# Entry of a two-block transformer kernel: the input rows and the first weight block in other pieces, and another order of the first roundings

## The reference

```
def rms_norm(x, g):
    y = xf * lax.rsqrt(jnp.mean(xf * xf, axis=-1, keepdims=True) + EPS)
    return (y * g.astype(jnp.float32)).astype(x.dtype)

def swiglu(h, w_gate, w_up, w_down):
    return (jax.nn.silu(h @ w_gate) * (h @ w_up)) @ w_down

x = x + 0.5 * swiglu(rms_norm(x, ffn1_norm[l]), ffn1_w_gate[l], ffn1_w_up[l], ffn1_w_down[l])
```

## Time and profile before

| what | value |
|---|---|
| median of 3 runs | 2433.48 us |
| profiled execution: its time, its span | 2435.74 us, 2434.0 us |
| TensorE busy | 2372.3 us, 97% |
| GpSimd, ScalarE, VectorE busy | 47%, 35%, 34% |
| share of TensorE in the chain that ended last | 88% |

### The profile page before, as it was taken

The page is one execution under the profiler, slowest core; times in us unless marked ns, Lnnn a source line. Parts: engine busy times, 40 slices in busy tenths (PEclk is TensorE's granted clock), DMA queues, the critical chain, the costliest instruction groups (busy, mean ns, idle before and its releaser), DMA issues.

```text
span 2434.0 us, 27037 instructions
## 1 busy us (share of the span) xinstructions
PE 2372.3 (97%) x11178; PEld 1930.8 (79%) x11178; DVE 821.5 (34%) x1415; ACT 855.4 (35%) x1260; POOL 1148.8 (47%) x936
## 2 busy tenths in 40 slices
PE   8999999999999999999997899999999899999999
PEld 6888887888877888888884678888876678788887
DVE  3222205754222221201568542021048864410210
ACT  4222215414343322213446443133165353531330
POOL 6444446525655444444551364444456521644443
PEclk9999999999999999999999999999999899999999
DMA  4323223212332332233230032332222201322232
GB/s 146 102 89 104 88 103 107 89 48 87 121 104 75 98 99 92 87 105 103 71 103 19 18 104 87 104 92 96 95 78 70 69 1 49 91 92 98 87 104 86
DMA packets 147132, 210.65 MB, mean 87 GB/s; under 512 B 6201, under 2 KB 112962, under 8 KB 147010
## 3 DMA queue, kind: packets, MB, share of 16 engines
q1 hardware_dynamic: 147010, 208.93, 26.7%
HBM read 206.82 MB, written 2.10 MB: 86 GB/s over the span
## 4 chain that ended last, share of the span: by engine, by line
PE 88%; DVE 7%; ACT 2%; issue 2%; DMA 1%; POOL 0%; SPq 0%; DVEq 0%; ACTq 0%
PE ps L1400 27%; PE ps L1402 26%; PE ps L1401 26%; PE ps L2157 1%; DVE c_work L2856 1%; DVE c_best L2855 1%; PE ps L2133 1%; PE ps L2143 1%; DVE hl L2292 1%; PE ps L1719 1%; PE ps L1741 1%; PE ps L1651 1%; DVE small L2716 0%; PE ps L2079 0%; DVE c_w L2662 0%
## 5 line engine op out<-in xcount | busy, mean ns | idle before, releaser
L757 POOL TENSOR_TENSOR wlo<-raw,whi 128x512 fp32r<-128x512 f32 x776 | 1010.2, 1335 | 1123.8 <-ACT whi L895 1007.5
L895 ACT ACTIVATE whi<-raw 128x2048 fp32r<-128x2048 f32 x189 | 360.1, 1905 | 699.6 <-DMA raw<-in_mlp_w 319.6
L1400 PE MATMUL ps<-hh,whi 128*128 128x512 f32 x1448 | 573.3, 396 | 6.9 <-DVE hl L2292 4.9
L1401 PE MATMUL ps<-hl,whi 128*128 128x512 f32 x1448 | 566.8, 391 | 0.0
L1402 PE MATMUL ps<-hh,wlo 128*128 128x512 f32 x1448 | 566.6, 391 | 0.0
L1400 PEld LDWEIGHTS ps<-hh,whi 128*128 128x128 f32 x1448 | 273.7, 189 | 75.5 <-DVE hl L2292 9.0
L1402 PEld LDWEIGHTS ps<-hh,wlo 128*128 128x128 f32 x1448 | 273.7, 189 | 57.8
L1401 PEld LDWEIGHTS ps<-hl,whi 128*128 128x128 f32 x1448 | 273.8, 189 | 56.9 <-issue 1.2
L1400 PE MATMUL ps<-gh,whi 128*128 128x512 f32 x736 | 286.3, 389 | 0.0
L1401 PE MATMUL ps<-gl,whi 128*128 128x512 f32 x736 | 286.3, 389 | 0.0
L1402 PE MATMUL ps<-gh,wlo 128*128 128x512 f32 x736 | 286.3, 389 | 0.0
(11 more groups left out here) (435 smaller groups left out, 2923.2 us busy)
## 6 DMA issues: line engine op xcount, KB each, us to landing
raw<-in_mlp_w SPq DMA_DIRECT2D x64, 1024.0 KB, 5.5
raw<-in_ffn_w_up SPq DMA_DIRECT2D x22, 1024.0 KB, 5.1
raw<-in_ffn_w_down SPq DMA_DIRECT2D x22, 1024.0 KB, 4.8
raw<-in_ffn_w_gate SPq DMA_DIRECT2D x21, 1024.0 KB, 5.1
raw<-in_w_in SPq DMA_DIRECT2D x13, 1024.0 KB, 5.2
raw<-in_diff_w_in SPq DMA_DIRECT2D x12, 1024.0 KB, 5.0
raw<-in_xattn_w_kv SPq DMA_DIRECT2D x8, 1024.0 KB, 4.9
raw<-in_dsa_w_in SPq DMA_DIRECT2D x8, 1024.0 KB, 5.0
```

Of the source, the lines that this page charges most:

```text
L757: nc.gpsimd.tensor_tensor(wlo[i][:, c], raw[i][:, c], whi[i][:, c].bitcast(F32), ALU.subtract).then_inc(s_lo, 1)
L895: nc.scalar.activation(whi[i][:, 0:width(made[0])], raw[i][:, 0:width(made[0])], ACT.Copy)\
L1400: nc.tensor.matmul(dst, w_hi, x_hi, start=start, stop=False)
L1401: nc.tensor.matmul(dst, w_hi, x_lo, start=False, stop=False)
```

## The change

SyncE sends x columns 0 to 255 (512 KB), the first half of block 0, x columns 256 to 511 (512 KB), the second half of block 0, and then x columns 512 to 1023 (1 MB). TensorE turns tiles 0 to 3 before block 0, tile 4 ahead of its k = 2, tiles 5 and 6 ahead of k = 3, tile 7 ahead of k = 4. ScalarE makes the quarters of `whi` of block 0 one at a time, makes the `hh` before the squares, and block 1's `whi` behind the `hh` of tile 7; the `whi` of block 3 moves ahead of the logarithm. GpSimd makes `wlo` of block 1 ahead of its addition t = 2 and that of block 2 ahead of t = 4. `square_total` moves from block 1 (ahead of k = 6) to block 2 (ahead of k = 6). Nothing of VectorE's program changes.

```
-            for h in range(2):
-                sp.dma_start(xrows[:, :, ts(h, 512)],
-                             dram["x"][0].rearrange("(t p) d -> p t d", p=P)[:, :, ts(h, 512)])\
-                    .then_inc(s_xin[h], 16)
+            x_in = dram["x"][0].rearrange("(t p) d -> p t d", p=P)
             for h in range(2):
+                sp.dma_start(xrows[:, :, ts(h, 256)], x_in[:, :, ts(h, 256)]).then_inc(s_xin[h], 16)
                 sp.dma_start(raw[0][:, ts(h, 1024)].rearrange("p (k n) -> p k n", n=256), first[:, 4 * h:4 * h + 4, :])\
                     .then_inc((s_rawa, s_raw[0])[h], 16)
+            sp.dma_start(xrows[:, :, 512:1024], x_in[:, :, 512:1024]).then_inc(s_xin[2], 16)
@@ square_sum (GpSimd)
-                    if t == 4:
+                    if b == 0 and t in (2, 4):
+                        split_to(t // 2)
+                    elif t == 4:
                         split_to(b + 1)
@@ ScalarE
+            def first_block(q):
+                act.wait_ge((s_rawa, s_raw[0])[q // 2], 16)
+                nc.scalar.activation(whi[0][:, ts(q, 512)], raw[0][:, ts(q, 512)], ACT.Copy).then_inc(s_hi0, 1)
+            def first_high(t):
+                act.wait_ge(s_x, t + 1)
+                nc.scalar.activation(hh[:, t, :], xT[:, t, :], ACT.Copy, scale=entry_gain(SWIGLU1, t)).then_inc(s_eh, 1)
+            def first_square(t):
+                if t >= 4:
+                    act.wait_ge(s_eacc, max(t - 4, 1))
+                nc.scalar.activation(sg[:, t % 4, :], xT[:, t, :], ACT.Square).then_inc(s_esq, 1)
+            def first_entry():
+                first_block(0)
+                first_high(0)
+                first_high(1)
+                first_block(1)
+                first_high(2)
+                first_high(3)
+                first_block(2)
+                first_square(0)
+                first_square(1)
+                first_high(4)
+                first_block(3)
+                first_high(5)
+                first_high(6)
+                first_square(2)
+                first_high(7)
+                prep_to(1)
+                for t in range(3, KT):
+                    first_square(t)
+                    if t == 5:
+                        prep_to(2)
+                prep_to(3)
@@ TensorE
+            def turn_first(t):
+                if t == 7:
+                    pe.wait_ge(s_par, 1)
+                if t in (0, 2, 4):
+                    pe.wait_ge(s_xin[t // 2], 16)
+                for st in range(ST):
+                    r = nc.tensor.transpose(ps[:, t, ts(st, P)], xrows[:, st, ts(t, P)], ident[:, :])
+                r.then_inc(s_tr0, 1)
+            def turn_pair():
+                turn_first(5)
+                turn_first(6)
@@ ffn, first block of a pair
-                             between={4: lambda: turn_residual(x0, 0)} if last_first else None)
+                             between={4: lambda: turn_residual(x0, 0)} if last_first else
+                             {2: lambda: turn_first(4), 3: turn_pair, 4: lambda: turn_first(7)} if p.b == 0 and r == 0
+                             else {6: lambda: square_total(p)} if p.b == 0 and r == 1 else None)
@@ ffn, second block of a pair
-                             between={3 if p.b else 6: lambda: square_total(p)} if head else
+                             between={3: lambda: square_total(p)} if head and p.b else
                              {3: lambda: turn_residual(x0, 1)} if last_first else None)
@@ ahead of the first layer
-            for t in range(KT):
-                if t == 7:
-                    pe.wait_ge(s_par, 1)
-                if t % 4 == 0:
-                    pe.wait_ge(s_xin[t // 4], 16)
-                for st in range(ST):
-                    r = nc.tensor.transpose(ps[:, t, ts(st, P)], xrows[:, st, ts(t, P)], ident[:, :])
-                r.then_inc(s_tr0, 1)
+            for t in range(4):
+                turn_first(t)
```

More of the change, by code:

```diff
@@ L345, in two_blocks @@
         s_hi0 = sem("s_hi0")
-        s_xin = [sem("s_xin0"), sem("s_xin1")]
+        s_xin = [sem("s_xin0"), sem("s_xin1"), sem("s_xin2")]
         s_raw = [sem("s_raw0"), sem("s_raw1"), sem("s_raw2")]
@@ L920, in entry @@
                 for t in range(KT):
[L921 to L924, removed]
                     act.wait_ge(s_x, 8 * (p.upd - 1) + t + 1)
-                    if t == 0 and p.b:
+                    if t == 0:
                         act.wait_ge(s_used, p.free)
@@ L940, in ffn @@
                     nc.scalar.preload_act_table_set(LN_SET)
-                    entry(p)
+                    if p.b:
+                        entry(p)
+                    else:
+                        first_entry()
                     prep_to(p.b + 2)
```

## The result

The changed kernel takes 2443.73 us, the median of six runs (2438.94 to 2446.43), beside 2433.89 for the kernel before in the same runs: a ratio of 1.0036, 95% interval 1.0025 to 1.0046. The medians lie 9.8 us apart; the ratio makes it 8.8 us (6.1 to 11.2). The forecast was 2.4 us, and the range went to 2439.5. The profiled execution took 2443.49 us.

What follows compares the result with a forecast made beforehand. TensorE, busy 97% of the span, was taken to bound the kernel. Block 3's 0.7 us later start plus 1.7 us of slow clock made +2.4 on 2433.5: 2435.9 us, range 2431.5 to 2439.5.

Steps and rivals of the forecast that it cites:

- its own sign: Before block 3: forecast wrong if TensorE's pause is missing, or block 3 begins before 51 or after 55 us.
- (one): Block 3, faster: the parameters' copy doesn't hold it, so 6.4 us stay won, total 2427.1 us; chance 6%.
- (two): Block 3, slower: it stays at 1.2 GHz, 6.6 us in place of 1.7, +7.3, total 2440.8 us; chance 7%.
- (four): Block 0: the early start doesn't come, it starts at 12.49 us again, chain 3.1 later, total 2439.0 us; chance 5%.
- rival three: Block 0: VectorE becomes its bound, every `hl` at 1.49 us, +2.2, total 2438.1 us; chance 10%.
- Loads: x at the entry: tiles 0 and 1 land 1.3 us sooner, at 4.9; tiles 2 and 3 at 7.55 us.
- The rule that I weighed and left out: x's loads: transfers under 1 MiB move more slowly, 3.9 us growing by a quarter or more, forecast by about 1 us.
- Block 0: First block: starts at 9.4 us, not 12.49, ends at 22.2; slow first matmuls taken as 0, up to 0.8 us.
- Block 1's start: Between blocks 0 and 1: TensorE waits 0.7 us for the first `wlo` quarter and starts at 22.9 us.
- Block 3 gives it back: Before block 3: copy ends 10.7 us behind the sum, at 52.8; 7.1 us pause, start at 52.85, 0.7 later than before.
- The slow clock: Start of block 3: slow matmuls behind the pause cost 1.7 us, bounds 0 and 6.6.
- +0.7 and +1.7: Block 3: 0.7 us later start and 1.7 us of slow matmuls, summed to +2.4 us.

Runs made afterwards that it cites:

- the filled pause: The changed kernel with 30 TensorE matmuls, their result unread, put into the pause before block 3: 2438.73 us, ratio 1.002 to the kernel before.
- the second set: The changed kernel, unaltered, run again beside the kernel before on one chip: 2441.59 us (9 runs), 8.5 us over it, ratio 1.0037.

## Why the prediction was wrong

The mechanism was right, and the place: the pause is where it was forecast, with the parameters' copy last before it, and the clock at 0.50 behind it. What failed is the size of terms. Slow matmuls at the start of block 0 were put at 0 and cost 2.1 us; the slow clock at block 3 was put at 1.7 us and cost 2.8; x's second landing came 0.9 us late. By its own sign too (block 3 before 51 or after 55) the forecast was missed: block 3 began at 56.07, 54.62 and 56.73 in three traces. No rival came instead: the copy did hold block 3 (one), block 3 ran at full pace after 6.1 us (two), and block 0 started at 10.04, not at 12.49 (four); three is answered below.

- **Loads.** "Tiles 2 and 3 (1.57 MB) land at 7.55": 8.42. The rate of 0.40 MB/us came from x in megabytes. From 4 to 8 us the changed kernel moved 341 and 329 GB/s (370 and 373, 356 and 339 in its other traces), the kernel before 397 and 399:

```profile
4.00:6.00 2.00, 1.00 1.05 341
6.00:8.00 2.00, 1.00 1.01 329
```

  The rule that I weighed and left out, that smaller transfers move more slowly (the Trainium skill, DMA: Bandwidth & Descriptors, section Bandwidth), had the sign right, with a price of 0.9 us in this trace against the estimate of 1. Rows of 1 KB instead of 2 KB come with the smaller transfers; the runs don't part the two. Over seven traces with these loads and no idle transposes between, tiles 2 and 3 landed between 8.3 and 9.9 us; with whole megabytes x landed at 6.3 to 6.4.
- **Block 0.** "Loses up to 4 x 0.2 = 0.8; I take 0": the first ten matmuls were slow, 12 took 4.8 us (10.04 to 14.88) instead of 2.7, 2.1 us. I had taken the pace of the kernel before at 12.49, and there the transposes had run with a break of 0.26 us. Here TensorE stood idle for 1.62 us between its two batches. The forecast had the eight transposes just ahead at the slow pace (7.55 to 9.4) and the matmuls behind them at the full one, without a reason for the change. The idle break is not the whole cause: behind 16 transposes in a row (whole megabytes) two or three matmuls were slow. The start at 10.04 instead of 9.4 and 0.6 us of small gaps make the rest of the 3.4 us by which block 0 ends late; the sum starts at 45.08, 3.0 later than the 42.1 forecast. `hl` held next to nothing (one gap of 0.15 us, at 21.16), as walked: rival three did not come.
- **Block 1's start.** TensorE waited 0.25 us for `wlo`, with 0.7 forecast.
- **Block 3 gives it back.** "10.7" us from sum to copy: 10.7. Block 3 started at 56.07, not at 52.85. That is the sum's 3.0 and the 0.25 us from the copy's end to the first matmul, where I had put 0.05.
- **The slow clock.** "I take 1.7": 14 matmuls at 0.43 us. They cost 2.8 us against the filled pause, and 3.1 against block 3 of the kernel before. In the earlier trace rows nine followed a pause of 4.0 us. The counts of 14, 10 and 14 in three traces of the same kernel say that it is no fixed price; my bounds of 0 and 6.6 held it. The 6 to 14 of the Trainium skill (TensorE: Matmul & The Clock Gate, Part 1), that stood beside it, would have been the better range.

So +0.7 and +1.7 were +3.9 and +3.1, 7.0 instead of 2.4 in this trace. The difference of the medians is 9.8, and 8.5 in the second set. Between these and the 6.4 of the three traces some 2 to 3 us stay unexplained, inside the intervals (6.1 us is their lower end); more slow stretches later in the kernel could be up to 1.7 of them, which is not shown. The range was too narrow, since I let the small terms of the beginning stand at their good end, though each microsecond there goes straight through the sum into block 3.

## What to carry to other kernels

When an operation moves later, list what is ordered behind it on every other engine, down to the small copy at the end of a pass; a wait that was met early gives no sign in a profile until its chain moves. A copy that frees a bank belongs right behind the write that it waits for. And an early start of a dense engine is worth what the next fixed wait leaves of it: here blocks 0 to 2 won 3.3 us and block 3 asked for 10.3.

## What was not expected of the hardware

- Idle work before the first load took the start of block 0 from slow to full pace (eight transposes 1.09 us instead of 1.97). A break of 1.62 us between two batches of transposes was followed by ten slow matmuls; in other executions, with breaks of 1.4 to 3.1 us, there were three to ten, without order: behind 3.1 us three in one trace and seven in another.
- A pause of 7.2 to 7.5 us was followed by 14, 10 and 14 slow matmuls in the changed kernel, 10 with x in whole megabytes and 13 with the moved sum alone.
- Executions of the kernel before spread over 9 to 16 us in sets of 21 to 32, and their time goes with the mean granted clock, from 2437.7 us at 0.989 to 2430.2 at 0.994 on the mean. A gain of 1 to 5 us in an entry is not seen in a handful of times. A trace shows it, but one trace is little too: the end of block 3 differed by 2.1 and 2.8 us between traces of one kernel.
- When the sum was back in block 1, two of VectorE's three steps of refinement took 1.67 us each beside GpSimd's `wlo`, and 0.69 where GpSimd was idle, so the copy ended at 49.5 us instead of the 47.5 expected:

```profile
40.65 1.67 DVE L2304 TENSOR_TENSOR t<-t 128x512 f32<-128x512 f32 x1
42.35 1.67 DVE L2305 SCALAR_TENSOR_TENSOR rstd<-t,rstd 128x512 f32<-128x512 f32 x1
```

  The Trainium skill (SBUF — State Buffer, section Who interferes with whom) has such pairs exclude each other; a whole GpSimd piece of 1.3 us was not added to each step, 1.0 us was.
